# Sparse attention inside a decoder trunk: the two head groups in alternation, compressed values in 120 rows

## The reference, cut to what matters

```python
k_cmp = rms_norm(compress(k_c, ...), k_norm_g)      # 15 compressed keys for each group
v_cmp = compress(v_c, cmp_pe_v, cmp_v_w1, cmp_v_w2)  # gelu(blk @ w1) @ w2
...
s_c = jnp.einsum('bqghd,bcgd->bghqc', qb, k_cmp) * SCALE
p_c = masked_softmax(s_c, cmp_end[None, :] <= t[:, None])
o_c = jnp.einsum('bghqc,bcgd->bqghd', p_c.astype(qb.dtype), v_cmp)
...
o_s = jnp.einsum('bghqnl,bgqnld->bqghd', p_s, vg)   # selected blocks: all of them here
o_w = jnp.einsum('bghqk,bkgd->bqghd', p_w.astype(qb.dtype), vw)
return gb[..., 0:1] * o_c + gb[..., 1:2] * o_s + gb[..., 2:3] * o_w
```

## Time and profile before

| | |
|---|---|
| median of 3 runs | 2606.54 us (2604.39 to 2607.41) |
| the profiled execution | 2600.24 us |
| its span, first to last instruction | 2598.3 us |
| granted TensorE clock, mean | 0.991 |
| TensorE busy | 98% of the span |
| DVE, ACT, POOL busy | 61%, 51%, 31% |

### The profile page before, as it was taken

One profiled execution on the slowest core, in us unless ns is written; L12 is line 12 of the kernel. 1 busy time (PEld: TensorE's weight loads), 2 busy tenths in 40 slices (PEclk: granted clock), 3 DMA queues, 4 the chain that ended last, 5 costly groups with the idle time before them and its releaser, 6 DMA issues.

```text
span 2598.3 us, 43985 instructions
## 1 busy us (share of the span) xinstructions
PE 2538.6 (98%) x18106; PEld 2339.7 (90%) x18106; DVE 1581.2 (61%) x2551; ACT 1319.4 (51%) x1937; POOL 798.8 (31%) x436
## 2 busy tenths in 40 slices
PE   7999999999999999999999999998999999999999
PEld 7898899999999998878798888998999999988887
DVE  6877667399244555555667775673992445555555
ACT  5486564344544444445544865643445454444444
POOL 0001210078888840000000112100888888300000
PEclk9999999999999999999999999999999999999999
DMA  6533235445544445566545322453455444455555
GB/s 232 192 117 114 82 117 186 145 152 183 178 146 139 141 164 192 194 214 227 178 163 188 118 101 82 133 198 116 163 187 177 141 140 146 164 193 194 195 194 170
DMA packets 95381, 419.27 MB, mean 161 GB/s; under 512 B 10704, under 2 KB 11088, under 8 KB 77776
## 3 DMA queue, kind: packets, MB, share of 16 engines
q1 hardware_dynamic: 95184, 416.46, 47.6%
HBM read 415.37 MB, written 1.05 MB: 160 GB/s over the span
## 4 chain that ended last, share of the span: by engine, by line
PE 92%; DVE 4%; DMA 2%; ACT 1%; POOL 1%; issue 0%; SPq 0%; DVEq 0%
PE bank L1929 25%; PE bank L349 18%; PE bank L351 18%; PE bank L350 18%; PE bank L1910 4%; PE bank L702 2%; DMA xr<-in_xstream 1%; PE bank L668 1%; PE bank L685 1%; PE bank L706 1%; DVE ring_lo L340 1%; POOL xr_lo L1641 1%; PE bank L1779 1%; PE bank L719 1%; PE bank L798 1%; PE bank L811 1%
## 5 line engine op out<-in xcount | busy, mean ns | idle before, releaser
L1636 ACT ACTIVATE xr_hi<-xr 128x1024 fp32r<-128x1024 f32 x512 | 542.2, 1060 | 790.3 <-DMA xr<-in_xstream 790.2
L1641 POOL TENSOR_TENSOR xr_lo<-xr,xr_hi 128x1024 fp32r<-128x1024 f32 x256 | 620.2, 2427 | 440.7 <-ACT xr_hi L1636 440.3
L349 PE MATMUL bank<-featH,xr_hi 128*128 128x256 f32 x2048 | 588.2, 287 | 10.0 <-POOL xr_lo L1641 10.0
L350 PE MATMUL bank<-featL,xr_hi 128*128 128x256 f32 x2048 | 576.6, 282 | 0.0
L351 PE MATMUL bank<-featH,xr_lo 128*128 128x256 f32 x2048 | 576.5, 282 | 0.0
L1641 DVE TENSOR_TENSOR xr_lo<-xr,xr_hi 128x1024 fp32r<-128x1024 f32 x256 | 313.6, 1226 | 305.1 <-ACT xr_hi L1636 304.9
L349 PEld LDWEIGHTS bank<-featH,xr_hi 128*128 128x128 f32 x2048 | 387.5, 189 | 11.2 <-issue 10.5
L350 PEld LDWEIGHTS bank<-featL,xr_hi 128*128 128x128 f32 x2048 | 387.5, 189 | 0.0
L351 PEld LDWEIGHTS bank<-featH,xr_lo 128*128 128x128 f32 x2048 | 387.2, 189 | 0.0
L349 PE MATMUL bank<-featH,ring_hi 128*128 128x256 f32 x1216 | 351.5, 289 | 9.2 <-DVE ring_lo L340 6.1
L350 PE MATMUL bank<-featL,ring_hi 128*128 128x256 f32 x1216 | 345.9, 284 | 0.0
(11 more groups left out here) (333 smaller groups left out, 4142.5 us busy)
## 6 DMA issues: line engine op xcount, KB each, us to landing
xr<-in_xstream SPq DMA_DIRECT2D x512, 512.0 KB, 3.3
ring<-in_wstream SPq DMA_DIRECT2D x128, 1024.0 KB, 4.9
first<-in_wstream SPq DMA_DIRECT2D x4, 1024.0 KB, 7.0
smw<-in_small SPq DMA_DIRECT2D x2, 1234.0 KB, 11.7
subk<-in_subkeys SPq DMA_DIRECT2D x2, 1024.0 KB, 8.2
x<-in_x SPq DMA_DIRECT2D x2, 512.0 KB, 6.6
big<-in_mix_row SPq DMA_DIRECT2D x2, 512.0 KB, 5.9
g_row<-in_ffn_row SPq DMA_DIRECT2D x2, 512.0 KB, 3.6
```

The source lines that it names most:

```text
L349: PE.matmul(o, s_hi_lo[0], m_hi_lo[0], start=first, stop=False)
L350: PE.matmul(o, s_hi_lo[0], m_hi_lo[1], start=False, stop=False)
L1636: A.activation(xr_hi[:, m % XR], xr[:, m % XR], ACT.Copy).then_inc(s_xhi, 1)
L1641: (PO if m < NKEY else V).tensor_tensor(xr_lo[:, m % XR], xr[:, m % XR], xr_hi[:, m % XR].bitcast(F32), ALU.subtract).then_inc(s_xlo_pool ...
```

## The change

Four things, in both layers:

1. In `scores`, the loops over group and branch are exchanged: the products now alternate between the two groups.
2. In `attend`, the products with the selected and window values alternate between the groups as well, and the two products with the compressed values come last.
3. The compressed probabilities of a query block are transposed eight heads at once, 120 columns (8 x 15) in one transpose, two transposes in turn(0) and turn(8) and none in the others. `pcT` then holds a block of queries, 120 rows, and ACT copies it once for each t.
4. The product with the compressed values has 120 rows: `vcmp` is [120, 4, 2, 64], the 15 rows repeated 8 times and all set to zero but those of the head. For it ACT repeats the turned hidden values 8 times (`chV`, four copies), the products with `w2` of the values get 120 columns of weights, and DVE writes `vcmp` by two multiplications with a mask (C_HEAD, 8 more columns of constants).

In the built program L706's product of 15 rows is placed in a tile of 32 rows x 64 columns; its successor with 120 rows is in one of 128 rows x 64 columns, as L702's products are. L636's products of 15 weight columns are in tiles of 128 rows x 32 columns, those of 120 weight columns in the full 128 x 128.

```diff
-                    vcmp = sb("vcmp", [NCMP, 2 * DH], F32, mid)
+                    vcmp = sb("vcmp", [8 * NCMP, 4, G, DH], F32, mid)
...
+                    chV = xb_flat[:, 2048:2048 + 4 * 8 * NCMP].rearrange("p (k g r c) -> p k g r c", k=2, g=G, r=8)
...
-                        for j in range(2):
-                            for g in range(G):
-                                for k in range(2):
-                                    mm = PE.matmul(bank[6][0:NCMP, (2 * j + g) * DH:(2 * j + g + 1) * DH],
-                                                   chT[:, 2 * j + k, g * 16:g * 16 + NCMP], w2[:, j, k, :],
-                                                   start=(k == 0), stop=(k == 1))
+                        for g in range(G):
+                            for k in range(2):
+                                PE.matmul(bank[6][0:NCMP, g * DH:(g + 1) * DH], chT[:, k, g * 16:g * 16 + NCMP], w2[:, 0, k, :],
+                                          start=(k == 0), stop=(k == 1))
+                        for g in range(G):
+                            for k in range(2):
+                                mm = PE.matmul(bank[6][0:8 * NCMP, (2 + g) * DH:(3 + g) * DH],
+                                               chV[:, k, g].rearrange("p r c -> p (r c)"), w2[:, 1, k, :],
+                                               start=(k == 0), stop=(k == 1))
                         mm.then_inc(s_co, 1)
...
-                            for g in range(G):
-                                for b in range(2):
+                            for b in range(2):
+                                for g in range(G):
                                     mm = PE.matmul(bank[2 + g][:, b * nk:(b + 1) * nk],
...
                             for k in range(t + 1):
                                 for j in range(4):
-                                    PE.transpose(bank[4 + k][:, j * P:(j + 1) * P], sc[:, n % 2, j, k * P:(k + 1) * P], ident)
-                            for g in range(G):
-                                tr = PE.transpose(bank[7][0:NCMP, g * P:(g + 1) * P], pc[:, 2 * i + g, 0:NCMP], ident)
+                                    tr = PE.transpose(bank[4 + k][:, j * P:(j + 1) * P], sc[:, n % 2, j, k * P:(k + 1) * P], ident)
+                            if i == 0:
+                                pe.wait_ge(s_cp, past(s_cp) + t + 1)
+                                if t:
+                                    pe.wait_ge(s_pcev, past(s_pcev) + 1)
+                                for h in range(2):
+                                    tr = PE.transpose(bank[7][0:8 * NCMP, h * P:(h + 1) * P],
+                                                      pc[:, 8 * h:8 * h + 8, :].rearrange("p h c -> p (h c)"), ident)
                             tr.then_inc(s_pt, 1)
...
+                            o = [bank[6][g * DH:(g + 1) * DH, (n % 4) * P:(n % 4 + 1) * P] for g in range(G)]
+                            for b, c in enumerate((VS, VW)):
+                                for k in range(t + 1):
+                                    for g in range(G):
+                                        PE.matmul(o[g], tok_kv[:, k, c + g * DH:c + (g + 1) * DH],
+                                                  pTk[k][:, n % 2, (2 * g + b) * P:(2 * g + b + 1) * P],
+                                                  start=b == 0 and k == 0, stop=False)
                             for g in range(G):
...
-                                mm = PE.matmul(o, vcmp[:, g * DH:(g + 1) * DH], pcT[:, n % 2, g * P:(g + 1) * P],
+                                mm = PE.matmul(o[g], vcmp[:, i % 4, g, :], pcT[:, t, i // 4 * P:(i // 4 + 1) * P],
                                                start=False, stop=True)
...
+                        for k in range(2):
+                            for g in range(G):
+                                at = (2 + k) * CROWS + 16 * g
+                                rep = A.activation(chV[:, k, g], times(bank[7][:, at:at + NCMP], 8), ACT.Copy)
+                        rep.then_inc(s_chtev, 1)
...
-                            A.activation(pcT[:, n % 2, :], bank[7][0:NCMP, 0:2 * P], ACT.Copy).then_inc(s_ptev_a, 1)
+                            t, i = units[n]
+                            if i == 0:
+                                A.activation(pcT[:, t, :], bank[7][0:8 * NCMP, 0:2 * P], ACT.Copy).then_inc(s_pcev, 1)
...
-                        dch.add(V.tensor_copy(vcmp[:], bank[6][0:NCMP, P:2 * P]))
+                        own = cst[0:8 * NCMP, C_HEAD:C_HEAD + 8].rearrange("p (a g) -> p a g", g=G)
+                        for g in range(G):
+                            dch.add(V.tensor_tensor(vcmp[:, :, g, :], times(bank[6][0:8 * NCMP, (2 + g) * DH:(3 + g) * DH], 4),
+                                                    over(own[:, :, g], DH), ALU.mult))
```

More of the change, by code:

```diff
@@ new lines @@
+    "lru_root": 2, "lru_split": 1, "merge_sigmoid": 3, "merged_split": 4, "norm_gain_loaded": 16, "norm_root": 2,
+    "one_hots": 64, "one_hots_weighted_act": 64, "one_hots_weighted_pool": 64, "out_first_tokens": 3, "pads_zero": 2,
+    "probsT_taken_act": 16, "probsT_taken_dve": 8, "probs_hi": 64, "probs_lo": 64, "probs_scaled": 16,
+    "probs_turned": 16, "qT_taken": 4, "q_root": 2, "q_squares": 2, "q_turned": 4, "q_turned_by_position": 2,
+    "row_exp": 16, "row_max": 16, "rows_loaded": 16, "scores": 16, "scores_taken": 32, "segsum": 8, "small_loaded": 16,
@@ L150, in constants @@
     c[:, C_IOTA:C_IOTA + NKEY] = np.arange(NKEY)
+    c[:, C_HEAD:C_HEAD + 8] = k // NCMP == np.arange(8)[None, :]
     return c
@@ L948, in mixer_scalar @@
                         act.wait_ge(s_cht, past(s_cht) + 1)
-                        A.activation(chT[:], bank[7][:, 0:4 * CROWS].rearrange("p (j c) -> p j c", j=4), ACT.Copy).then_inc(s_chtev, 1)
+                        A.activation(chT[:], bank[7][:, 0:4 * CROWS].rearrange("p (j c) -> p j c", j=4), ACT.Copy)
+                        for k in range(2):
[3 more added lines that the diff above has]
+                        rep.then_inc(s_chtev, 1)
                         filler(XBC + 1)
```

67 lines of the change are left out of this document (28 added, 39 removed).

## The result

| | before | after |
|---|---|---|
| median of the runs | 2606.91 us (4 runs, 2604.39 to 2607.41) | 2561.14 us (4 runs, 2557.68 to 2564.96) |
| ratio | | 0.9825, 95% interval 0.981 to 0.9841 |
| profiled execution, its span | 2600.24, 2598.3 us | 2564.96, 2563.2 us |
| granted TensorE clock, mean | 0.991 | 0.988 |

The time got better in the way forecast and by more than forecast, so the question behind the experiments is which terms of the sum were mis-sized.

What follows compares the result with a forecast made beforehand. TensorE was taken to bound the kernel. Passages 6.4, transposes 3.1 and attend's overlap 9.8, less 1.1 for the compressed values, gave 18.2 us a layer, 36.4 in both: forecast 2570 us, range for 8 in 10 2563 to 2591.

Steps and rivals of the forecast that it cites:

- What bounds the kernel: Whole span, attention included: TensorE busy 98%; a microsecond of its work removed saves one unless another engine is late.
- Switches of tile: In attend, three of four passages between value and 15-row tiles vanish, 0.14 us each: 6.4 us a layer.
- Alternation in attend: Value products of alternating groups run side by side: 0.47 and 0.85 us a unit, 9.8 us a layer.
- The staircase: In attend, one product's second record runs beside the next's first: n products take n + 1 slots, not 2n.
- Rival B: In attend, group 1 queues behind group 0 at 0.109 us a record, so alternation gains nothing: 2590 us, chance 0.27.
- Alternation in the scores: Exchanging the score loops gains nothing, since a product there is already a pair of records running together.
- Compress stage: Making the 120-row compressed values costs TensorE 0.4 and DVE 0.5 us, nothing hiding it: -1.1 us a layer.
- Waits: TensorE's wait before turn(15) grows from 0.50 to about 1.8 us; the two at 245.30 and 248.43 stay.
- The sum: Tile passages 6.4, transposes 3.1, attend's overlap 9.8, compressed values -1.1: 18.2 us a layer, 36.4 in both.
- C: The scores' products overlap as well, saving 3.3 us a layer more: 2563 us, chance 0.12.
- D: In attend each change of column tile costs a passage of 0.14 us: slower, 2621 us, chance 0.06.
- E: DVE holds the shorter units, or half-clock stretches fall otherwise; half of alternation's gain lost: 2580 us, chance 0.07.

Runs made afterwards that it cites:

- experiment 4: Kernel before, with only attend's order changed: value products alternate between groups, both 15-row compressed products last; 2569.87 us, ratio 0.9861.
- experiment 5: Kernel before, with only the two 15-row compressed products moved to the end of attend, groups not alternating; 2574.12 us, ratio 0.9882.
- experiment 1: Changed kernel, but all of group 0's value products before group 1's, both compressed products still last; 2564.03 us, ratio to before 0.984.
- Experiment 11: Changed kernel with group 1's score products left out; 2564.24 us in its one run.
- Experiments 10: Changed kernel with group 1's selected and window value products left out, both compressed products kept; 2556.43 us in its one run.
- experiment 2: Changed kernel with attend in its old order, each group's value products followed by its compressed one; 2571.93 us, ratio to before 0.9868.
- experiment 3: Changed kernel with the scores in their old order, group 0 twice, then group 1 twice; 2559.66 us, ratio to before 0.9819.
- experiment 7: Changed kernel with DVE's two multiplications of the compressed values done four times over, eight in all; 2564.65 us, ratio to before 0.9847.
- 9: Changed kernel with DVE's two multiplications of the compressed values done twice over, four in all; 2561.93 us in its one run.

## Why the prediction was wrong, step by step

**What bounds the kernel: right.** TensorE is the chain before and after, and TensorE work taken out of the attention came off the span.

**Switches of tile: right.** 0.14 us a passage, read from the gaps in the earlier trace rows, is what lies between experiment 4 and the changed kernel (0.95 to 0.81, 1.39 to 1.25), and between 5 and 1 (0.96 to 0.81, 1.88 to 1.73).

**Alternation in attend: the step that failed.** This is the largest part of the miss. "Then n products take n + 1 slots rather than 2n" and the 0.01 us added at every overlap gave 0.47 and 0.85 us a unit, 9.8 a layer. (Its arithmetic slipped besides: 0.01 us at 5 and 9 overlaps leaves 0.50 and 0.89. That would have given 10.2, and even without any offset 11.2.) Measured: attend lost 1.07 and 1.50 us, of which 0.43 are the three passages, so the overlap gave 0.64 and 1.07, 8 x 0.64 + 7 x 1.07 = 12.6 a layer, 2.8 more than forecast. Twelve records take 6 slots of 0.109 us and twenty take 10: two whole products of different groups lie side by side, not the tail of one and the head of the next. The staircase came from the reading of the scores ("A product there is already a pair of records that run together"). Experiment 11 refutes that reading: a product's two records follow each other in the scores as they do in attend, and what runs together are the two groups. Read so, the half-height rows would have given the full factor: two groups, half the time.
The Trainium skill, "TensorEngine Tiling (Array Packing)", Tiling Modes, states that tiles work independently and load and multiply in parallel. Experiments 10 and 11 agree with it (1.25 to 1.24 us with four of attend's ten products gone, and 1.06 to 1.06 with two of the scores' four), and it was the prediction that set the wrong row against it. Its other rule, that a change of mode drains the array and a change of tile does not, agrees too: 0.14 us at each change of size, none at a change of group.

**Rival B, "group 1 queues behind group 0": wrong, and its evidence was misread.** That the records of the earlier trace rows came one by one was no sign that the halves cannot overlap. The 15-row product stood between the groups, and experiments 2 and 5 show the groups overlapping without alternation once it has the same tile or is out of the way. That is also why the alternation proper was worth little: 0.48 us in the second half's units and nothing in the first's (experiment 1 against the changed kernel).

**Alternation in the scores: right value, wrong reason.** Nothing was taken and nothing came (experiment 3), but because the groups already overlapped, not because such an overlap gives nothing.

**Compress stage: the second step that failed, "nothing hides it".** Forecast -1.1 us a layer, measured -0.25. The sizes were right. TensorE's part was +0.4 us: the unit behind the products starts 1.41 us after the first of them (121.50 to 122.91) and started 0.99 after it (119.22 to 120.21). DVE starts 0.54 us later after the first product than before (1.64 and 1.10), and its two multiplications take 0.76 us where the copy took 0.28. These 0.54 and 0.48 are just the 1.0 us by which its idle time before the reciprocal shrank, from 1.66 to 0.66: DVE's part is hidden behind ACT, which the earlier trace rows did not hold, since they show DVE and TensorE only. Of TensorE's 0.4, 0.15 us fell into the slack at 126.40. Experiments 7 and 9 show how far the cover reaches.

**Waits: mostly right.** The one before turn(15) was to grow to 1.8 and is 2.01, since attend(14) shrank by more; the one before turn(8) stayed at 1.8. Not foreseen: DVE's 0.75 us at 248.43 does not show after, because a stretch at half clock now lies on it (in experiments 3 and 9, without that stretch, it is back at 0.75), and the wait for ACT behind turn(15) fell from 0.55 to 0.30.

**The sum.** Compressed scores to turn(15), forecast 17.7: eight and six units with 0.17 and 0.22 us more overlap give 2.7, the covered wait 0.75, together 21.2, as measured. Behind turn(15), forecast 1.5: 0.22 and 0.25 more, 1.97 against 1.92. The compress stage 0.85 less. All of it is 4.8 us a layer over the forecast, 9.5 in both, and the miss is 8.9 (2570.0 to 2561.1). Of the 4.8, the overlap is 2.9, the compress stage 0.85, and 1.0 are the two waits; the 0.75 among them was in hand only because a stretch at half clock fell on it, and is no merit of the change.

**Rivals C to E:** C gave nearly the right time (2563), but by luck: it had the scores gain 3.3 us a layer, and they gained nothing, since they overlapped already. D needed a cost at each change of column half, and there is none. Of E, DVE did not become the bound; half-clock stretches did fall otherwise in the profiled execution, but cost the medians nothing like its 10 us.

## What to carry to other kernels

Look for what stands between two jobs that could share the array, before you interleave them: one product of another tile size between two groups cost this kernel 30 us (experiment 5), by its passages (2 x 0.14 us a unit, some 9 us) and for the rest by keeping the second group from starting. In this kernel products of the same tile size on different halves overlapped by themselves when no more than about four records lay ahead; leaving one half's products out is the quickest test of whether they do. And before a new instruction is put on the path of a short chain across engines, follow that chain through every engine, table loads too: what is taken for the path may have idle time in it (here 1.66 us of DVE's).

## What was not expected of the hardware

- TensorE started a product of one column half ahead of up to four records of the other that stood before it. In three programs of different order the second half began when four records of the first were left (experiments 1, 2 and 10). Whether the limit is in products, records or queue entries was not tried; all products here leave two records.
- In the old order the groups did not overlap across the 15-row product. That it is the change of tile size which holds them apart fits experiments 2 and 5: a product of the same size at that place (experiment 2) does not hold them apart, nor does the 15-row product behind both groups (5). A short product in the large tile was not tried, so the number of rows itself stays a possible cause.
- A wait of 1.67 us of TensorE (experiment 7) was followed by 3.4 us at a clock of 0.51, which raised its price from 1.74 to 3.24 us. Not every wait was followed so: in the changed kernel the one of 1.81 us before turn(8) was (237.7 to 241.1) and the one of 2.01 before turn(15) was not; in experiments 3 and 9 it was the other way round.
